# Two transformer blocks on one core: attention outputs turned in the bank of their group's values, in pieces two units apart

## What is computed

```python
for i in range(DEPTH):
    h_lat = modulate(rms_norm(x, norm_mix[i]), sh1, sc1)
    h_ctx = modulate(rms_norm(ctx, norm_mix[i]), csh1, csc1)
    if i % 2 == 0:    # window + neighbourhood attention, 16 heads, for latents and context
        y_lat, y_ctx = even_mixer(h_lat, h_ctx, ...)
    else:             # latent attention, 16 heads over 768 keys, for the latents
        y_lat, y_ctx = odd_mixer(h_lat, h_ctx, ...)
    x = x + g1 * y_lat
    x = x + g2 * squared_relu_mlp(...)
```

## Times and profile before

| what | value |
|---|---|
| median of 3 runs | 4327.04 us (4322.94 to 4331.87) |
| profiled execution | 4322.1 us, span 4320.5 us |
| TensorE busy | 3914.2 us, 91% of the span |
| VectorE busy | 2263.0 us, 52% |
| ScalarE busy | 1536.5 us, 36% |
| mean granted clock of TensorE | 0.955 of full speed |

### The profile page before, as it was taken

How to read it: one execution, slowest core, us unless ns; L and a number is a source line. 1 busy time by engine, 2 the same in 40 slices (tenths; PEclk the granted TensorE clock), 3 DMA queues, 4 the chain that set the end, 5 groups by cost and what they waited for, 6 DMA issues and landing times. The chain is left out here.

```text
span 4320.5 us, 52368 instructions
## 1 busy us (share of the span) xinstructions
PE 3914.2 (91%) x19042; PEld 3185.2 (74%) x19042; DVE 2263.0 (52%) x4038; ACT 1536.5 (36%) x2638; POOL 125.4 (3%) x188
## 2 busy tenths in 40 slices
PE   5999978999899997899969998699999679898999
PEld 3887766888688776688848887588888457576887
DVE  3665564666566566366643345245555444444555
ACT  2222453222322335322245555232221454543222
POOL 1000000000100000000000000000000000000000
PEclk9999989999999998999989999899999889998999
DMA  6443202443544320244311110112121100002332
GB/s 242 134 136 102 64 25 73 137 131 117 179 131 136 98 66 23 78 137 131 112 52 49 54 40 16 54 54 63 58 63 34 55 29 1 25 1 78 95 96 77
DMA packets 98987, 350.86 MB, mean 81 GB/s; under 512 B 11043, under 2 KB 14627, under 8 KB 97912
## 3 DMA queue, kind: packets, MB, share of 16 engines
q1 hardware_dynamic: 75768, 271.50, 20.4%
q0 software_dynamic: 18304, 70.33, 5.0%
q10 hardware_dynamic: 4736, 6.62, 0.4%
HBM read 342.59 MB, written 11.06 MB: 82 GB/s over the span
## 5 line engine op out<-in xcount | busy, mean ns | idle before, releaser
L174 DVE TENSOR_TENSOR w_lo<-w_raw,w_hi 128x1024 fp32r<-128x1024 f32 x494 | 607.0, 1230 | 1165.6 <-ACT w_hi L167 1165.2
L167 ACT ACTIVATE w_hi<-w_raw 128x1024 fp32r<-128x1024 f32 x494 | 523.0, 1060 | 1867.1 <-PE ps L198 1699.1
L196 PE MATMUL ps<-h_hi,w_hi 128*128 128x512 f32 (+1 forms) x2824 | 1094.1, 387 | 66.6 <-DVE h_lo L255 35.0
L197 PE MATMUL ps<-h_lo,w_hi 128*128 128x512 f32 (+1 forms) x2824 | 1082.3, 383 | 0.0
L198 PE MATMUL ps<-h_hi,w_lo 128*128 128x512 f32 (+1 forms) x2824 | 1081.5, 383 | 0.0
L196 PEld LDWEIGHTS ps<-h_hi,w_hi 128*128 128x128 f32 x2824 | 537.2, 190 | 194.0 <-issue 54.9
L198 PEld LDWEIGHTS ps<-h_hi,w_lo 128*128 128x128 f32 x2824 | 537.2, 190 | 103.2
L197 PEld LDWEIGHTS ps<-h_lo,w_hi 128*128 128x128 f32 x2824 | 538.6, 191 | 100.1 <-issue 1.4
L196 PE MATMUL ps<-a_hi,w_hi 128*128 128x512 f32 x1472 | 548.8, 373 | 3.3 <-DVE ctx_x L454 3.3
L197 PE MATMUL ps<-a_lo,w_hi 128*128 128x512 f32 x1472 | 547.0, 372 | 0.0
L198 PE MATMUL ps<-a_hi,w_lo 128*128 128x512 f32 x1472 | 545.9, 371 | 0.0
(11 more groups left out here) (253 smaller groups left out, 4500.6 us busy)
## 6 DMA issues: line engine op xcount, KB each, us to landing
w_raw<-in_w_first SPq DMA_DIRECT2D x316, 512.0 KB, 3.6
w_raw<-in_w_mlp SPq DMA_DIRECT2D x128, 512.0 KB, 3.6
shared<-in_w_ada POOLq DMA_DIRECT2D x96, 512.0 KB, 4.3
w_raw<-in_w_even SPq DMA_DIRECT2D x26, 512.0 KB, 3.7
w_raw<-in_w_odd SPq DMA_DIRECT2D x24, 512.0 KB, 3.7
near_stage<-near_bias POOLq DMA_DIRECT2D x32, 256.0 KB, 2.9
bias_rows<-bias_line SPq DMA_DIRECT2D x1, 5120.0 KB
shared<-silu_cond POOLq DMA_DIRECT2D x4, 1024.0 KB, 5.0
```

The source lines that it names most:

```text
L167: act.activation(self.hi[:, n % H, :], self.raw[:, n % R, :], ACT.Copy).then_inc(self.hi_done, 1)
L174: dve.tensor_tensor(self.lo[:, n % self.n_hl, :], self.raw[:, n % self.n_raw, :], self.hi[:, n % self.n_hl, :].bitcast(F32), ALU.subtract) ...
L196: pe.matmul(out, lhs[0], rhs[0], start=start, stop=False)
L197: pe.matmul(out, lhs[0], rhs[1], start=False, stop=False)
```

## The change

The turn of a group is made in pieces of four blocks, one every second step: piece p of group g in step 8g + 9 + 2p. A piece is transposed into bank 6 + g % 2, which held the group's values and has been normalised by then. ScalarE makes its high parts in the same step as before; VectorE makes the low parts one step later, after the bias of that step. The second piece waits on TensorE for the low parts of the first, since both use one bank. The wait for all probability copies before a turn is gone, and so is the wait of each batch of probability transposes for the low parts. The first values of a group now wait for the low parts of the pieces that used its bank. Turns behind the last unit alternate between banks 6 and 7, and their low parts are made in the same step.

```diff
+                self.turn_steps, self.turned_by, n = {}, {}, 0
                 for g in sorted(turns):
-                    self.turn_at[min(8 * g + 8, len(units) - 1)] = g
-                    self.turn_n[g] = n
-                    n += len(turns[g]) // 4
+                    for p in range(len(turns[g]) // 4):
+                        at, bank = 8 * g + 9 + 2 * p, 6 + g % 2
+                        if 8 * g + 8 >= len(units):
+                            at, bank = len(units), 6 + (g + p) % 2
+                        self.turn_steps.setdefault(at, []).append((g, p, bank, n))
+                        n += 1
+                    self.turned_by[g] = n
...
-                def turn(g):
+                def turn(g, p, bank, k):
                     pe.wait_ge(self.out_done, g + 1)
-                    for c in range(0, len(self.turns[g]), 4):
-                        if turns_done[0] >= 2:
-                            pe.wait_ge(self.chunk_lo, turns_done[0] - 1)
-                        for j in range(4):
-                            m = pe.transpose(ps[:, 4 + turns_done[0] % 2, 128 * j:128 * j + 128],
-                                             self.turns[g][c + j][0], ident[:, :])
-                        m.then_inc(self.chunk_turned, 1)
-                        turns_done[0] += 1
+                    if k:
+                        pe.wait_ge(self.chunk_lo, k - (bank != 6 + g % 2))
+                    for j in range(4):
+                        m = pe.transpose(ps[:, bank, 128 * j:128 * j + 128], self.turns[g][4 * p + j][0], ident[:, :])
+                    m.then_inc(self.chunk_turned, 1)
...
                             pe.wait_ge(self.by_dve if t % 2 else self.by_act, self.evacs(t - 1, t % 2))
-                        if turns_done[0]:
-                            pe.wait_ge(self.chunk_lo, turns_done[0])
...
                     if u % 8 == 0 and g >= 2:
                         pe.wait_ge(self.out_done, g - 1)
+                        if g - 2 in self.turned_by:
+                            pe.wait_ge(self.chunk_lo, self.turned_by[g - 2])
...
-                    if u - 1 in self.turn_at:
-                        copied(min(u, len(units) - 1))
-                        turn(self.turn_at[u - 1])
+                    for step in self.turn_steps.get(u, ()):
+                        turn(*step)
...
-                    if u - 1 in self.turn_at:
-                        g = self.turn_at[u - 1]
-                        for c in range(0, len(self.turns[g]), 4):
-                            k = self.turn_n[g] + c // 4
-                            act.wait_ge(self.chunk_turned, k + 1)
-                            for j in range(4):
-                                m = act.activation(self.turns[g][c + j][1], ps[:, 4 + k % 2, 128 * j:128 * j + 128],
-                                                   ACT.Copy)
-                            m.then_inc(self.chunk_hi, 1)
+                    for g, p, bank, k in self.turn_steps.get(u, ()):
+                        act.wait_ge(self.chunk_turned, k + 1)
+                        for j in range(4):
+                            m = act.activation(self.turns[g][4 * p + j][1], ps[:, bank, 128 * j:128 * j + 128], ACT.Copy)
+                        m.then_inc(self.chunk_hi, 1)
...
-                    if u - 1 in self.turn_at:
-                        g = self.turn_at[u - 1]
...
+                    for g, p, bank, k in (*(self.turn_steps.get(u - 1, ())),
+                                          *(self.turn_steps.get(u, ()) if u == len(units) else ())):
+                        dve.wait_ge(self.chunk_hi, k + 1)
+                        for j in range(4):
+                            hi, lo = self.turns[g][4 * p + j][1:]
+                            m = dve.tensor_tensor(lo, ps[:, bank, 128 * j:128 * j + 128], hi.bitcast(F32), ALU.subtract)
+                        m.then_inc(self.chunk_lo, 1)
```

More of the change, by code:

```diff
@@ L553, in __init__ @@
                 self.sinks_before = [sum(g["minus_sinks"] is not None for g in groups[:k]) for k in range(len(groups) + 1)]
-                self.turn_at, self.turn_n = {}, {}
-                n = 0
+                self.turn_steps, self.turned_by, n = {}, {}, 0
                 for g in sorted(turns):
-                    self.turn_at[min(8 * g + 8, len(units) - 1)] = g
-                    self.turn_n[g] = n
-                    n += len(turns[g]) // 4
+                    for p in range(len(turns[g]) // 4):
[5 more added lines that the diff above has]
+                    self.turned_by[g] = n
                 self.turn_total = n
@@ L574, in tensor @@
                 tmp, units = self.tmp, self.units
-                turns_done = [0]
                 ready(pe)
```

## The result

| | before | after |
|---|---|---|
| median of 4 runs | 4325.62 us (4322.94 to 4331.87) | 4256.27 us (4252.99 to 4258.2) |
| profiled execution | 4322.1 us, span 4320.5 | 4252.99 us, span 4251.4 |

The ratio of the times is 0.9837, with a 95% interval of 0.982 to 0.9854: 69.4 us less by the medians, 69.1 by the profiled executions. The forecast was 4263 in a range of 4242 to 4292.

The account below looks back on a forecast made before the run. TensorE, busy 91% of the span, was taken to bound the kernel. Gains of 80.9 us less 1.0 and 17.9 gave 62.0, so 4322.1 became 4260; 3 us carried over made 4263, range 4242 to 4292.

Parts of the forecast that it names:

- The stall: 17 turns inside attentions: probability transposes no longer wait for the low parts, minus 46.5 us.
- the copies' wait: Before a turn, TensorE's wait for the last copies of the probabilities goes: minus 2.7 us.
- The clock: Five stretches holding all 17 turns inside attentions: TensorE's granted clock returns to full speed, worth 31.7 us (29 to 34).
- The rival in which it falls at each of 28 pieces: TensorE's clock drops at every piece after the change; at 3.3 us each 30 us slower, 4355 us; chance 0.05.
- The odd layer: Six turns of one piece: nothing more added, as ScalarE and VectorE have room; unit with a piece about 3.8 us.
- The long units of the even layer: Three turns of two pieces there: 0.3 us a turn added, plus 1.0 us, bounds 0 to 5.
- The short units: Eight turns among units with two blocks of keys: 1.65 us a piece, 3.3 a pair, 17.9 us added.
- The series: Among units with two blocks of keys, ScalarE's 0.76 and VectorE's 0.89 us add up: 1.65 us a piece.
- the two kinds of gap: TensorE gaps near pieces among units with two key blocks: values waiting for ScalarE's copy, probability transposes for the exponential.
- the new wait: TensorE at unit 8g+16, values waiting for low parts: costs nothing, since these are done some four units earlier.
- The sum: Whole kernel: 80.9 us removed less 1.0 and 17.9 added gives 62.0 us gain.
- The median: Runs' median lay 4.9 us above the profiled execution; 3 us carried over, turning 4260 into 4263.

## Why the prediction was right, and by how much it was off

**The stall** (46.5 us) and **the copies' wait** (2.7 us): both gone, as the two lists above show. The bank frees TensorE, which the kernel with the bank alone shows in the odd layer.

**The clock** (31.7 us): 30.3 and 31.7 by the fillers. This was the term most open to doubt, and multiplying the missing share of clock by TensorE's busy share was accurate. The rival in which it falls at each of 28 pieces is refuted: the clock is 1.00 in all five stretches.

**The odd layer** (nothing more): the turn's step is 3.68 us, where about 3.8 was named. VectorE's low parts (0.88 us, 3556.87) start as soon as its bias ends and push the copy to 3557.67; nobody is late. **The long units of the even layer** (0.3 us a turn): nothing; the step with a piece is 3.14 us (2463.30 to 2466.44) against 2.69 (2469.13 less 2466.44), 0.45 more, which is the 0.44 us of the transposes in the odd layer and nothing else:

```profile
2463.30 0.71 PE L609 MATMUL ps<-ident,arena 128*128 128x128 f32 x5
...
2466.00 0.61 PE L598 MATMUL ps<-ident,arena 128*128 128x128 f32 x4
...
2466.44 0.71 PE L609 MATMUL ps<-ident,arena 128*128 128x128 f32 x5
...
2469.13 0.72 PE L609 MATMUL ps<-ident,arena 128*128 128x128 f32 x5
```

**The short units** (3.3 us for a pair of pieces): the first turn of the first block lengthens the seven steps from its own on to 11.08 us; the same steps, with the clock kept up by the matmul filler and the stalled one counted as an undisturbed 1.05 us, take 7.88. So 3.2 us there, and 2.8 and 2.4 at the second and third turn. The series was the right picture, and a little too dear. Of the two kinds of gap that were named, one came: in the rows of the changed kernel above, the values wait 0.39 us for ScalarE's copy behind the high parts, and in the first attention such waits of the values are 6 with 2.23 us, where before there was none. The other didn't: the probability transposes there wait for the exponential 7 times, 1.75 us, against 7 times, 1.72 us before. Nor do the values wait for low parts anywhere, the new wait that was put at nothing.

**What was mis-sized.** The sum was 62.0 us, the profiled executions say 69.1. The clock was right, so the miss is in the rest, 30.3 us forecast. Against the kernel with matmul fillers, which has the old waits at a full clock, the changed kernel gains 37.8 us in the attentions, 7.5 more than forecast. By steps, in round numbers:

- A pair of pieces among short units was taken at 3.3 us and costs 2.4 to 3.2, at eight turns 3.8 us in all.
- The transposes of a piece were taken to cost the same before and after, 0.53 to 0.60 us by their rows. Behind the old turn TensorE stood still, so the row's full 0.60 us was paid; in the stream of the changed kernel the next transposes start 0.44 us after the turning ones do (3553.14 to 3553.58), though the row is still 0.60 long. This is 0.16 us for each of the nine turns in the odd layer and among long units, 1.4 us in all.
- The 0.3 us for each of the three long turns were not needed, 1.0 us.
- The last 1.3 us or so are in the stalled steps of the short units: in the first block they lie 4.26 to 4.68 us above an undisturbed one, where the waits and transposes of the rows make 4.29. What the difference is no row shows.

All four misses have the same sign. The stall itself was read rightly: the stalled step of the odd layer is 6.17 - 3.24 = 2.93 us too long, which is 2.33 us of waiting and 0.60 of transposes. What the rows of the old kernel didn't tell is how much of the 0.60 stays when nothing stands still behind it.

**The median**: I carried 3 of 4.9 us over from the profiled execution, and the changed kernel's median is 3.3 us above its profiled execution. The forecast is 6.7 us above the median: 7.1 too little gain, less 0.3 of offset.

What stays open: how the clock's fall depends on the length or the place of an idle time; three of the 17 stalls before had none behind them, and nothing here says why.

## To carry to other kernels

Here a helper step that borrowed a buffer of the main pipeline cost the main engine its whole latency through both engines it visits. Give such a step a buffer that is free at that time, and put as many steps between two uses of that buffer as the helper's chain takes. Look at what follows a stall as well as at the stall: here the half clock behind 46.5 us of waiting cost another 31. And where an engine has little free time, both the place of the helper's instructions and their number count: making the low parts one step later was worth some 8 us in the attentions beside what the clock gave, merging four instructions into one 4.9 us, a wider distance another 3.5.

## What the runs showed of the hardware

Filling an idle TensorE with useless transposes made the old kernel 28 to 31 us faster by the medians (4324.7 to 4296.9 with transposes, to 4293.4 with matmuls); the stall itself stayed. What I had not expected is that identity transposes keep the clock up as fully as matmuls do: the attentions have 13.0 and 13.3 us at half clock, against 79.4 before.

A copy of four blocks of 128 columns as one instruction of 512 takes ScalarE 0.59 us against 0.76 to 0.79 for four, VectorE 0.69 against 0.88, with a strided output.

In two profiled executions of the very same kernel (three units apart) the stretches outside the attentions took 3637.9 and 3647.9 us. The difference goes with the time at half clock there, 301 and 329 us. Differences under some 10 us between kernels are therefore better read from the stretch that was changed than from the whole time.
